# The scan's output made feature by feature, and turned back in the merge

## What is computed

```python
def step(S, inp):
    r_t, w_t, k_t, v_t, kk_t, kka_t = inp
    sa = jnp.einsum('bdhvk,bdhk->bdhv', S, kk_t)
    S = (S * w_t[..., None, :] - sa[..., :, None] * kka_t[..., None, :]
         + v_t[..., :, None] * k_t[..., None, :])
    return S, jnp.einsum('bdhvk,bdhk->bdhv', S, r_t)
...
y = ys[:, :, 0] + jnp.flip(ys[:, :, 1], axis=1)
mu = jnp.mean(y, axis=-1, keepdims=True)
var = jnp.mean(jnp.square(y - mu), axis=-1, keepdims=True)
yn = ((y - mu) * lax.rsqrt(var + GN_EPS)).reshape(B, T, C) * lnx_w.astype(f32) + lnx_b.astype(f32)
```

## Time and profile before

| what | value |
|---|---|
| three executions, median | 4115.06 us (4111.81 to 4118.41) |
| the profiled execution | 4123.43 us |
| its span, first to last instruction | 4121.5 us |
| mean granted TensorE clock | 0.946 |
| scan stage, by the trace | about 1034 to 2060 us of the span |
| merge stage, by the trace | about 2064 to 3350 us of the span |

### The profile page before, as it was taken

One profiled execution on the slowest core, in us unless ns is written; L12 is line 12 of the kernel. 1 busy time (PEld: TensorE's weight loads), 2 busy tenths in 40 slices (PEclk: granted clock), 3 DMA queues, 4 the chain that ended last, 5 costly groups with the idle time before them and its releaser, 6 DMA issues. The chain is left out here.

```text
span 4121.5 us, 63378 instructions
## 1 busy us (share of the span) xinstructions
PE 3679.3 (89%) x24950; PEld 2869.7 (70%) x24951; DVE 1216.3 (30%) x2285; ACT 749.1 (18%) x1399; POOL 1154.1 (28%) x1677
## 2 busy tenths in 40 slices
PE   8799999996688888989879999999999968999960
PEld 1566666664588888888869989899898954444430
DVE  0122222222344444444312222222222141222227
ACT  0122222221222232223201111111111101111113
POOL 0133333333556655665411011110111101000013
PEclk9899999998799999999989999999999978999985
DMA  7522222222333233223171111111111135675226
GB/s 246 201 85 88 85 85 86 85 77 91 94 98 88 63 95 98 85 66 95 38 265 62 40 59 37 39 62 39 51 46 39 67 105 184 225 256 189 93 97 214
DMA packets 272119, 424.40 MB, mean 103 GB/s; under 512 B 121998, under 2 KB 172820, under 8 KB 271894
## 3 DMA queue, kind: packets, MB, share of 16 engines
q1 hardware_dynamic: 250504, 348.24, 25.3%
q0 software_dynamic: 11952, 43.52, 3.2%
q10 hardware_dynamic: 9444, 29.30, 1.8%
HBM read 288.02 MB, written 132.98 MB: 102 GB/s over the span
## 5 line engine op out<-in xcount | busy, mean ns | idle before, releaser
L1701 PE MATMUL c_ps<-c_hT,big 128*128 128x128 f32 x6528 | 752.3, 276 | 25.9 <-DMA big<-in_w_in 25.9
L1701 PEld LDWEIGHTS c_ps<-c_hT,big 128*128 128x128 f32 x6528 | 743.6, 193 | 33.9 <-issue 30.6
L641 PE MATMUL a_ps<-a_win,a_hT 128*128 128x512 f32 (+1 forms) x1088 | 416.2, 540 | 3.6 <-DVE a_mix L561 3.6
L2124 PE MATMUL e_ps<-big,e_xT 128*128 x784 | 346.9, 596 | 2.3 <-DVE e_xT L2086 2.3
L635 PE MATMUL a_ps<-a_hT,a_win 128*128 128x128 f32 x2992 | 343.5, 277 | 1.6 <-ACT a_hT L385 1.6
L635 PEld LDWEIGHTS a_ps<-a_hT,a_win 128*128 128x128 f32 x2992 | 340.2, 193 | 5.6 <-issue 2.7
L641 PEld LDWEIGHTS a_ps<-a_win,a_hT 128*128 128x128 f32 x1088 | 204.0, 190 | 199.8 <-issue 187.0
L1037 POOL TENSOR_TENSOR b_tmp<-b_tt,b_ta 128x126 f32<-128x126 f32 (+22 forms) x527 | 203.1, 385 | 333.0 <-DMA b_ta<-s_a 277.7
L2124 PEld LDWEIGHTS e_ps<-big,e_xT 128*128 128x128 f32 x784 | 149.2, 191 | 191.3 <-issue 191.3
L1701 PE MATMUL c_ps<-c_wo,c_mT 128*128 128x512 f32 x544 | 236.3, 592 | 0.0
L1040 POOL TENSOR_TENSOR b_tt<-b_tt,b_tmp 128x126 f32<-128x126 f32 (+22 forms) x527 | 212.9, 404 | 41.3
(11 more groups left out here) (306 smaller groups left out, 5257.8 us busy)
## 6 DMA issues: line engine op xcount, KB each, us to landing
big<-in_exp_w SPq DMA_DIRECT2D x48, 1024.0 KB, 10.5
s_D<-a_oD SPq DMA_DIRECT2D x34, 768.0 KB, 5.9
b_f<-s_D SPq DMA_DIRECT2D x34, 768.0 KB, 7.8
s_yr<-e_yo ACTq DMA_DIRECT2D x49, 512.0 KB
m_w<-in_ada_w SPq DMA_DIRECT2D x12, 2048.0 KB, 8.1
b_f<-s_A SPq DMA_DIRECT2D x34, 512.0 KB, 6.0
s_A<-a_oA SPq DMA_DIRECT2D x17, 768.0 KB, 3.4
big<-in_w_in SPq DMA_DIRECT2D x12, 1024.0 KB, 12.3
```

The costliest lines, as they stand in the source:

```text
L641: ins = nc.tensor.matmul(ps[:, bank, 0:width], hT[b][:, k, :], win[:, k, c:c + width], start=k == 0, stop=k == KD - 1)
L1701: return nc.tensor.matmul(out, lhsT, rhs, start=start, stop=stop)
L2124: return nc.tensor.matmul(out, lhsT, rhs, start=start, stop=stop)
```

## The change

The scan makes y with features on partitions and tokens along the columns. The state `Shd` becomes stationary and `RT` moves. The values `V` and `Us` of one head become stationary tiles of 64 columns, the two heads of a pair writing partitions 0 to 63 and 64 to 127, and the mixing blocks `ArkT` and `ArbT` move with 128 columns. The copy, the stores and the loads keep their sizes. In the merge, PE turns the sum of both directions back with four transposes into WB[1] (`turn_y`), once ahead of the first tile for tile 0 and then after project(2) of each tile for the next one. DVE's `scan_center` reads that PSUM bank instead of `ya`, and PE waits for it (`yc_ok`) before it writes the bank again.

```diff
@@ stage_scan, tensor, step
                         for j in range(4):
-                            mm(bank(d, 1)[:, j * P:(j + 1) * P], RT[d][:, j, :], Shd[d][:, j, :], stop=False)
-                            for h in (2 * j, 2 * j + 1):
-                                own = slice(h * N, (h + 1) * N)
-                                mm(bank(d, 1)[:, own], ArkT[d][:, slot(h), :], V[d][b][:, own], start=False, stop=False)
-                                ins = mm(bank(d, 1)[:, own], ArbT[d][:, slot(h), :], Us[d][:, own], start=False, stop=h % 2 == 1)
+                            at = bank(d, 1)[:, j * P:(j + 1) * P]
+                            mm(at, Shd[d][:, j, :], RT[d][:, j, :], stop=False)
+                            for mix, val in ((ArkT, V[d][b]), (ArbT, Us[d])):
+                                for u in range(2):
+                                    h = 2 * j + u
+                                    ins = mm(at[64 * u:64 * u + 64], val[:, h * N:(h + 1) * N], mix[d][:, slot(h), :],
+                                             start=False, stop=mix is ArbT)
                         ins.then_inc(y_ps[d], 1)
@@ stage_merge, vector
                 def scan_center(t):
-                    after(dve, s["ysum"], t)
-                    v.reduce_sum(s8[0][:, :], by_head(ya[:, :]), axis=X_AXIS).then_inc(s["m_ok"], 1)
+                    after(dve, s["yt_ps"], t)
+                    v.reduce_sum(s8[0][:, :], by_head(ps[:, WB[1], :]), axis=X_AXIS).then_inc(s["m_ok"], 1)
...
-                    v.tensor_tensor(by_head(yb[:, :]), by_head(ya[:, :]), wide(s8[5][:, :]), ALU.subtract)\
+                    v.tensor_tensor(by_head(yb[:, :]), by_head(ps[:, WB[1], :]), wide(s8[5][:, :]), ALU.subtract)\
                         .then_inc(s["yc_ok"], 1)
@@ stage_merge, tensor
+                def turn_y(t):
+
+                    after(pe, s["ysum"], t)
+                    freed(pe, s["yT_ok"], t)
+                    for k in range(4):
+                        ins = nc.tensor.transpose(ps[:, WB[1], k * P:(k + 1) * P], ya[:, k * P:(k + 1) * P], ident)
+                    ins.then_inc(s["yt_ps"], 1)
+
+                turn_y(0)
+
...
                     after(pe, s["yf_ok"], t)
                     freed(pe, s["mix_ok"], t, 2)
+                    after(pe, s["yc_ok"], t)
...
                     for j in range(KD):
                         project(j)
+                        if j == 2 and left > 0:
+                            turn_y(t + 1)
                         if j + 4 < KD:
                             gates(j + 4)
...
                     for i in range(2):
                         freed(pe, s["mix_ok"], t, 2)
+                        if i == 1 and left > 0:
+                            after(pe, s["yc_ok"], t + 1)
```

More of the change, by code:

```diff
@@ L1433, in stage_merge @@
             "w_in", "wp_in", "wo_in", "pad_ok", "rp_in", "h_in", "cs_in", "y_in", "x_in", "ysum", "m_ok", "mean_ok", "yc_ok", "sq_ok",
-            "v_ok", "ve_ok", "sd_ok", "rs_ok", "yn_ok", "yw_ok", "yo_ok", "yf_ok", "yT_ps", "yT_ok",
+            "v_ok", "ve_ok", "sd_ok", "rs_ok", "yn_ok", "yw_ok", "yo_ok", "yf_ok", "yt_ps", "yT_ps", "yT_ok",
             "G_ps", "G_ok", "P_ps", "M_ok", "mg_ok", "W_ps", "mix_ok", "x2_ok", "ss_ok", "ms_ok", "sx_ok", "rx_ok",
```

## The result

The changed kernel takes 4130.49 us in the median of eight executions (4125.05 to 4142.89); the kernel before, run beside it, takes 4117.09 us (4109.29 to 4120.16). The ratio is 1.0037, with a 95% interval of 1.0025 to 1.0050. That is 15 us slower, between 10 and 21. The profiled execution took 4129.29 us with a span of 4127.5 us, 6.0 us longer than the span before.

A forecast was written before the change was run, and what follows sets the result against it. PE bounds the merge without holes, while a circle through POOL, SP and the DMA queue paces the scan. Scan -5, transposes +6.7, tile 0 0 and first `turn_y(t + 1)` +15.8 give +17.5 us: 4132.6 us, range 4119 to 4142.

The forecast's parts named there:

- The price of changing shape: Output y: time lost at each change of PE's tile shape; a pair takes 1.00 us, saving 0.12 us.
- The first rival: Scan's y block: PE's saving counts whole and shape changes are free, 62 us go against 22.5 added: 4075 us; 4%.
- the second: Scan: shape changes are free but the circle holds, 16 us saved: 4122 us, no measurable change; 7%.
- The fifth: Output y: passes don't pair, PE needs 2.6 us more a tile, scan +5 to +12: about 4145 us; 6%.
- Forecast -5 us: Scan: 2.6 us returned over some 14 steps plus 2.2 us whole in the last two tiles; between 0 and -19.
- the circle: Scan: a loop through POOL, SP and the DMA queue sets the step of 59.0 us, taking only `raw` from PE.
- The third rival: Scan: the price of shape changes holds but PE's saving counts whole, -19 + 22.5: 4119 us; 5%.
- a sixth: Scan: share of PE's saving that the circle returns, 0.5 of 2.9 us, so 0.2 us a step.
- One sign: Scan: PE's wait for the `u5` copy grows by about 1 us a step, steps still 58 to 59 us.
- 6.7 + 15.8: Merge: 15 x 0.45 us of transposes in tiles 2 to 16, plus tile 0's 13.2 us standstill, transposes and low clock.
- `turn_y(0)` was hidden, as costed: Merge, tile 0: gates(0) starts 2.8 us later, covered by gates(4)'s 3.08 us wait for weights; cost 0.
- the fourth rival: Merge, tile 0: PE doesn't stand still because y of tile 1 lands earlier, +2 us: 4117 us; 4%.

The follow-up runs named there:

- ACT's order alone: Kernel before, with ACT's `own_decay` moved behind its `u5` copies and nothing of the change: 4092.62 us, 0.9939 of the kernel before.
- the merge alone: Changed kernel with the old y lines in the scan, so only the merge is changed: 4134.89 us, 1.0044 of the kernel before.
- the grouped kernel: Changed kernel with tile 0's `turn_y(1)` after project(4) and y's products ordered by tile shape: 4109.82 us, 0.9984 of the kernel before.
- ACT's order: ACT's `own_decay` moved behind its `u5` copies, here in the kernel with y's products ordered by tile shape: 4092.32 us, 0.9945 of the kernel before.

## Why the prediction was right

Forecast were 4132.6 us, in a range of 4119 to 4142, and slower with 80%. Measured were 4130.49 us: +15 us (10 to 21) against +17.5.

- **Output y.** Forecast 1.00 us a pair from the spatial gating's rows, measured 1.005, and the eight passes need the same 0.59 us to the next shape (1186.41 - 1185.82). The block took 8.0 us, not 7.8: the first pair is only some 0.05 us shorter than the others (1186.41 - 1185.45 = 0.96), where 0.2 were counted, so a tile saves 0.93 us and not 1.1. The price of changing shape, which kept a gain of 0.67 down to 0.12 us a pair, was shown apart by grouping: 5.58 us a tile in place of 8.0. The first rival and the second, with free changes, fall. The fifth falls too, as eight passes do run two at a time.
- **The scan.** Forecast -5 us, measured alone -6.2 (-9.9 to -2.5). That the circle passes on only a part was shown by adding work (a fifth of 31 us came through), by grouping (a sixth of 41 us) and by ACT's order alone, where a `raw` that started 5.3 us sooner brought the next inverse forward by 0.3 us. The third rival, with PE's saving whole, falls. That the part was read as a sixth from two steps was luck, as steps scatter by more than those two differ; that it is small was not. One sign came weaker than stated: PE's wait for the `u5` copy was to grow by about 1 us a step and grew by (73.0 - 69.0) / 14 = 0.3. That is within the scatter of profiles: from 1130 to 1920 us the wait is 66.1 us in the kernel before and 61.7 in the merge alone, which have the same scan.
- **The merge's tiles and tile 0.** Forecast 6.7 + 15.8 = 22.5 us, and the trace shows 21.8 us from tile 0 to tile 16. The runs put the merge alone at +18 (13 to 24), which holds both. The standstill was 12.71 us where 13.2 were forecast. The transposes behind it cost 0.91 us and not 0.45, since they too ran at the lower clock, and gates(6) lost 7.43 - 5.52 = 1.9 us, where 2.1 were forecast: 12.71 + 0.91 + 1.9 = 15.5 us in all. So the parts were each off by up to half a us, and the errors nearly cancelled. `turn_y(0)` was hidden, as costed. Moving `turn_y(1)` by two projections brought 14 us back, so the fourth rival's condition, y of tile 1 in time, is what decides.
- **What was missed.** The prediction called the pace a circle through POOL, SP and the DMA queue, and took POOL's 29.4 us inverse as given. It is not: a part of it is POOL meeting DVE. This changed no term of the sum, since the change leaves that meeting in place (L1040 at 410 ns in the grouped kernel, 409 before), but it made the expectation for ACT's order too small.

## What to carry to other kernels

When an engine's order has no hole, look at each new wait for what stands behind it: here one wait of 12.7 us in the first of 17 tiles cost more than all the transposes together, and two projections ahead of it were enough to hide it. A swap of operands that halves the passes has to pay for each change of tile shape, so group by shape before counting on it. Where a circle sets the pace, PE's savings come back as a fraction; measure that fraction by adding work, and look at the durations inside the circle itself for operations that are long only because of a neighbour.

## What the runs showed of the hardware that was not expected

- A POOL operation of two SBUF inputs took 0.68 in place of 0.28 us beside a DVE operation of two SBUF inputs, and 0.29 us for nearly the same size beside one with an operand in PSUM. For an operation on 126 elements it was 0.93 in place of 0.41 us.
- Passes of the two 64-column halves ran side by side even where they were issued head by head: 1.01 us a pair in either order. The Trainium skill, page "TensorE: Matmul & The Clock Gate", section "Part 3: Packing small matmuls — row/col tiling", says that matmuls start and end strictly in the order of the program. The trace differs: all four passes of `V` start before those of `Us`, though a pass of `Us` stands between them in the program. Here the measurement decides.
- The same lines of scan took 957.4 us in one program's profiled execution and 948.3 us in another's, from the first operation of the first inverse to the last L1037 of the last one.
